# Three later norms of the residual: squares summed beside the residual's updates, root and inverse on [token, tile], reordering inside the dense stage

## The reference

```python
def _rmsnorm(x, g):
    x32 = x.astype(F32)
    y = x32 * lax.rsqrt(jnp.mean(x32 * x32, axis=-1, keepdims=True) + RMS_EPS)
    return y.astype(x.dtype) * g
def _modulate(h, shift, scale):
    return h * (1.0 + scale) + shift
...
    xl = xl + ml[2] * yl                                   # after the mixer
    hl = _modulate(_rmsnorm(xl, norm_g[i, 1]), ml[3], ml[4])
    xl = xl + ml[5] * ffn(hl)                              # after the feed-forward part
```

## Time and profile before

| | us |
|---|---|
| median of three runs | 2930.53 (2927.93 to 2930.65) |
| the profiled execution, its own time | 2932.93 |
| its span in the trace | 2930.9 |
| PE busy in the span | 2728.1 (93%) |
| DVE, ACT, POOL busy | 1048.0, 644.9, 520.1 |
| granted PE clock, mean | 0.958 |

### The profile page before, as it was taken

The page is one execution under the profiler, slowest core; times in us unless marked ns, Lnnn a source line. Parts: engine busy times, 40 slices in busy tenths (PEclk is TensorE's granted clock), DMA queues, the critical chain, the costliest instruction groups (busy, mean ns, idle before and its releaser), DMA issues. The chain is left out here.

```text
span 2930.9 us, 46270 instructions
## 1 busy us (share of the span) xinstructions
PE 2728.1 (93%) x18862; PEld 1829.9 (62%) x18863; DVE 1048.0 (36%) x2314; ACT 644.9 (22%) x1362; POOL 520.1 (18%) x466
## 2 busy tenths in 40 slices
PE   6699999796999999987999999999886999999997
PEld 6355555453555555554776677766635887688774
DVE  5244544416776664012444344443402110010100
ACT  0344544302222220004223232232102111010000
POOL 0111111003332224211333122331100010000000
PEclk6899999898999999998999999999887999999999
DMA  6142241202333333100111101110018997495731
GB/s 222 45 121 63 63 126 42 89 1 86 102 113 114 114 117 82 49 11 22 31 31 31 30 2 31 31 30 9 7 52 301 348 321 221 159 296 163 251 108 29
DMA packets 309234, 297.73 MB, mean 102 GB/s; under 512 B 5712, under 2 KB 268880, under 8 KB 308944
## 3 DMA queue, kind: packets, MB, share of 16 engines
q1 hardware_dynamic: 303024, 273.30, 30.4%
q0 software_dynamic: 4896, 17.83, 2.3%
q10 hardware_dynamic: 1152, 4.19, 0.4%
HBM read 281.14 MB, written 12.58 MB: 100 GB/s over the span
## 5 line engine op out<-in xcount | busy, mean ns | idle before, releaser
L1601 PE MATMUL bank<-work,weight_ring 128*128 128x128 f32 (+1 forms) x2048 | 315.4, 317 | 6.1 <-ACT work L1651 6.1
L2014 PE MATMUL bank<-hidden,weight_ring 128*128 128x512 f32 (+1 forms) x768 | 310.2, 538 | 1.8 <-ACT work L2336 1.8
L1601 PEld LDWEIGHTS bank<-work,weight_ring 128*128 128x128 f32 x2048 | 291.8, 193 | 27.7 <-issue 8.1
L601 PE MATMUL bank<-weight_ring,hidden 128*128 128x384 f32 x760 | 266.5, 495 | 4.9 <-ACT work L730 4.6
L1147 PE MATMUL bank<-hidden,weight_ring 128*128 128x384 f32 x704 | 238.2, 492 | 18.4 <-issue 18.4
L1268 DVE SCALAR_TENSOR_TENSOR weight_ring<-weight_ring,silu_c 128x256 f32<-128x256 f32 x308 | 217.8, 748 | 5.5
L601 PEld LDWEIGHTS bank<-weight_ring,hidden 128*128 128x128 f32 x760 | 137.9, 191 | 109.0 <-ACT work L730 16.6
L1147 PEld LDWEIGHTS bank<-hidden,weight_ring 128*128 128x128 f32 x704 | 133.1, 192 | 107.2 <-issue 20.6
L2014 PEld LDWEIGHTS bank<-hidden,weight_ring 128*128 128x128 f32 x768 | 135.5, 190 | 82.8 <-issue 68.7
L1147 PE MATMUL bank<-weight_ring 128*128 128x384 f32 x528 | 182.4, 496 | 0.3 <-DVE work L1276 0.3
L1756 DVE TENSOR_TENSOR work<-work,bank 128x128 f32<-128x128 f32 (+1 forms) x88 | 29.7, 337 | 426.0 <-ACT work L1656 426.0
(11 more groups left out here) (330 smaller groups left out, 3775.5 us busy)
## 6 DMA issues: line engine op xcount, KB each, us to landing
weight_ring<-in_moe_w_in SPq DMA_DIRECT2D x64, 1024.0 KB, 10.4
weight_ring<-in_ada_w SPq DMA_DIRECT2D x38, 1024.0 KB, 5.2
weight_ring<-in_ffn_w_in SPq DMA_DIRECT2D x44, 512.0 KB, 4.9
hidden<-in_moe_w_out SPq DMA_DIRECT2D x8, 2816.0 KB, 10.5
residual<-in_moe_w_out SPq DMA_DIRECT2D x8, 2816.0 KB, 16.1
work<-in_moe_w_in SPq DMA_DIRECT2D x16, 1024.0 KB, 8.8
weight_ring<-in_na_w_qkv SPq DMA_DIRECT2D x24, 512.0 KB, 7.7
weight_ring<-in_gdn_w_qkv SPq DMA_DIRECT2D x24, 512.0 KB, 5.4
```

The costliest lines, as they stand in the source:

```text
L601: mm = nc.tensor.matmul(m.psum[6][:, 0:3 * P], m.H[:, k, t * P:(t + 1) * P], weights(u)[:, k, :], start=(k == 0), stop=(k == KD - 1))
L1601: mm = nc.tensor.matmul(B[c % 4][:, ab * HALF:ab * HALF + N], w[:, ab, k, (c % 2) * P:(c % 2 + 1) * P], XG[:, k, 0:N], start=(k == 0), sto ...
L2014: mm = nc.tensor.matmul(B[b][:, c0:c0 + t1 - t0], W[:, s, k, :], m.H[:, k, t0:t1], start=(k == 0), stop=(k == KD - 1))
```

## The change

Norm n0 stays as it is. For n1, n2 and n3:

- ScalarE squares each group of the residual as soon as VectorE's additions to it are done, inside the projection's block or inside the dense stage. GpSimd adds the squares of groups 1 to 6 (in order of completion) to those of the first in `m.sq_sum`; the last group's squares stay in `m.sq`. Both are [128, 768]. They take the place of a buffer `silu_c_wide`, which now is a part of the same memory.
- `norm_apply` takes the place of `norm_modulate`. For each tile of 128 tokens TensorE makes two matmuls with the squares as the stationary operand and one column of 1/1024 as the moving one, so that the mean square of a token stands on its partition: [128, 6] for 768 tokens. ScalarE takes the root (after a one-element root at the start of the block), VectorE the inverse, both on [128, 6] ([128, 4] in n3). TensorE spreads each column over all partitions: stationary operand is the column, broadcast, and the moving one the identity. VectorE multiplies the residual by it, straight from PSUM and into `m.H`, and ScalarE scales and shifts `m.H` in place.
- `reorder` is gone. In the dense stage ScalarE copies each completed group's latents in the new order into `m.sq`, copies them back into the residual, and squares them from `m.sq`.

```diff
@@ -171,6 +171,8 @@
     m = Core()
...
     m.norm_sems = None
+    m.sq_sems = None
+    m.spread_sem, m.spread_base = None, 0
...
     m.sc = sb("silu_c", 2 * KD)[:, :]
-    m.sc32 = sb("silu_c_wide", 32 * KD)[:, :].rearrange("p (k v) -> p k v", k=KD)
+    stat = sb("square_sums", 2 * TOK)
+    m.sq_sum, m.sq = stat[:, 0:TOK], stat[:, TOK:2 * TOK]
+
+    m.sc32 = stat[:, 0:32 * KD].rearrange("p (k v) -> p k v", k=KD)
...
+def square_sums(m):
+    if m.sq_sems is None:
+        m.sq_sems = semaphores(m, "norm", "squared collected")
+        m.sq_base = [0, 0]
+    sems = m.sq_sems + m.sq_base
+    m.sq_base = [m.sq_base[0] + KD, m.sq_base[1] + KD - 2]
+    return sems
+def collect_squares(m, pool, sems, e, first=0):
+    squared, collected, squared_0, collected_0 = sems
+    pool.wait_ge(squared, squared_0 + e + 1)
+    if e > 1:
+        pool.wait_ge(collected, collected_0 + e - 1)
+    m.nc.gpsimd.tensor_tensor(m.sq_sum[:, first:TOK], m.sq_sum[:, first:TOK], m.sq[:, first:TOK], ALU.add).then_inc(collected, 1)
+def norm_apply(m, layer, norm, first=0, ahead=None):
+    nc = m.nc
+    if m.spread_sem is None:
+        m.spread_sem, = semaphores(m, "norm", "spread")
+    _, _, summed, root, inverted, scaled, hidden = m.norm_sems
+    _, _, summed_0, root_0, inverted_0, scaled_0, hidden_0 = m.norm_base
+    spread, spread_0 = m.spread_sem, m.spread_base
+    tiles = range(first // P, TOK // P)
+    rs = cut(m, 0, TOK // P)
+    warm = cut(m, TOK // P, 1)
+    parts = [(CTX, TOK, 0)] + ([(0, CTX, 1)] if first == 0 else [])
+    n = len(parts)
+    used = (0, 0, 1, 2, 1, KD * n, KD * n)
+    m.norm_base = [b + u for b, u in zip(m.norm_base, used)]
+    m.spread_base += n
+    with nc.Block() as block:
+        if ahead:
+            @block.sync
+            def _(sp):
+                ahead(sp)
+        @block.tensor
+        def _(pe):
+            for t in tiles:
+                for src in (m.sq_sum, m.sq):
+                    mm = nc.tensor.matmul(m.psum[0][:, t:t + 1], src[:, t * P:(t + 1) * P], const(m, C_MEAN, 1), start=(src is m.sq_sum),
+                                          stop=(src is m.sq))
+            mm.then_inc(summed, 1)
+            pe.wait_ge(inverted, inverted_0 + 1)
+            for b, (t0, t1, _) in enumerate(parts):
+                for t in range(t0 // P, t1 // P):
+                    mm = nc.tensor.matmul(m.psum[1 + b][:, t * P - t0:(t + 1) * P - t0], rs[:, t:t + 1].to_broadcast([P, P]), const(m, C_IDENT),
+                                          start=True, stop=True)
+                mm.then_inc(spread, 1)
+        @block.scalar
+        def _(act):
+            nc.scalar.activation(warm, const(m, C_EPS, 1), ACT.Sqrt).then_inc(root, 1)
+            act.wait_ge(summed, summed_0 + 1)
+            nc.scalar.activation(rs[:, first // P:], m.psum[0][:, first // P:TOK // P], ACT.Sqrt, bias=const(m, C_EPS, 1)).then_inc(root, 1)
+            for k in range(KD):
+                for b, (t0, t1, v) in enumerate(parts):
+                    act.wait_ge(scaled, scaled_0 + k * n + b + 1)
+                    nc.scalar.activation(m.H[:, k, t0:t1], m.H[:, k, t0:t1], ACT.Identity, bias=m.MOD[:, layer, 3 * norm, k, v:v + 1],
+                                         scale=m.MODA[:, layer, norm, k, v:v + 1]).then_inc(hidden, 1)
+        @block.vector
+        def _(dve):
+            dve.wait_ge(root, root_0 + 2)
+            nc.vector.reciprocal(rs[:, first // P:], rs[:, first // P:]).then_inc(inverted, 1)
+            for k in range(KD):
+                for b, (t0, t1, _) in enumerate(parts):
+                    dve.wait_ge(spread, spread_0 + b + 1)
+                    nc.vector.tensor_tensor(m.H[:, k, t0:t1], m.X[:, k, t0:t1], m.psum[1 + b][:, 0:t1 - t0], ALU.mult).then_inc(scaled, 1)
...
+    sums = square_sums(m)
+    squared, collected, _, collected_0 = sums
     with nc.Block() as block:
+
+        @block.scalar
+        def _(act):
+            for g in range(KD):
+                act.wait_ge(added, (g + 1) * len(parts))
+                if g > 1:
+                    act.wait_ge(collected, collected_0 + g - 1)
+                nc.scalar.activation((m.sq if g else m.sq_sum)[:, first:TOK], m.X[:, g, first:TOK], ACT.Square).then_inc(squared, 1)
+
+        @block.gpsimd
+        def _(pool):
+            for g in range(1, KD - 1):
+                collect_squares(m, pool, sums, g, first)
...
                 pool.wait_ge(*loaded(r, 1))
                 pool.wait_ge(product, out_done(r, "P2"))
                 nc.gpsimd.tensor_tensor(b, b, a, ALU.subtract).then_inc(weights_ok, 1)
+                for e in range(max(1, 2 * r - 2), 2 * r):
+                    collect_squares(m, pool, sums, e)
+            collect_squares(m, pool, sums, KD - 2)
...
                     nc.scalar.activation(sa[:, 1], sa[:, 1], ACT.Silu).then_inc(silu_ok, 1)
+
+
+            order = m.sq[:, CTX:TOK]
+            for e in range(KD):
+                r, row = divmod(e, 2)
+                g = r + PAIRS * row
+                act.wait_ge(added, len(OUT) * r + OUT.index(("P3", "P4")[row]) + 1)
+                if e > 1:
+                    act.wait_ge(collected, collected_0 + e - 1)
+                if e == 1:
+                    act.wait_ge(squared, sums[2] + 1)
+                at = 4 * FK + 4 + 2 * e
+                nc.scalar.copy(order.rearrange("p (r c) -> p r c", c=GRID_C), m.X[:, g, CTX:TOK].rearrange("p (c r) -> p r c", r=GRID_R))\
+                    .then_inc(copied, 1)
+                act.wait_ge(copied, at + 1)
+                nc.scalar.copy(m.X[:, g, CTX:TOK], order).then_inc(copied, 1)
+                act.wait_ge(copied, at + 2)
+                to = m.sq if e else m.sq_sum
+                nc.scalar.activation(to[:, CTX:TOK], order, ACT.Square)
+                nc.scalar.activation(to[:, 0:CTX], m.X[:, g, 0:CTX], ACT.Square).then_inc(squared, 1)
...
-def reorder(m):
-
-    nc = m.nc
-    copied, = semaphores(m, "reorder", "copied")
-    back, = semaphores(m, "reorder", "back")
-    tmp = cut(m, 0, KD * LAT).rearrange("p (k t) -> p k t", k=KD)
-    with nc.Block() as block:
-
-        @block.vector
-        def _(dve):
-            for k in range(KD):
-                nc.vector.tensor_copy(tmp[:, k, :].rearrange("p (r c) -> p r c", c=GRID_C),
-                                      m.X[:, k, CTX:TOK].rearrange("p (c r) -> p r c", r=GRID_R)).then_inc(copied, 1)
-
-        @block.scalar
-        def _(act):
-            for k in range(KD):
-                act.wait_ge(copied, k + 1)
-                nc.scalar.copy(m.X[:, k, CTX:TOK], tmp[:, k, :]).then_inc(back, 1)
...
         norm_modulate(m, "n0", 0, 0, ahead=attention_ahead(m))
         neighbourhood_attention(m, ahead=projection_ahead(m, "no", dram["na_w_o"]))
         project_to_residual(m, "no", 0, 0)
-        norm_modulate(m, "n1", 0, 1, ahead=swiglu_ahead(m))
+        norm_apply(m, 0, 1, ahead=swiglu_ahead(m))
         swiglu(m)
-        reorder(m)
-        norm_modulate(m, "n2", 1, 0, ahead=delta_net_ahead(m))
+        norm_apply(m, 1, 0, ahead=delta_net_ahead(m))
         delta_net(m)
         project_to_residual(m, "go", 1, CTX, load=projection_ahead(m, "go", dram["gdn_w_o"]))
-        norm_modulate(m, "n3", 1, 1, first=CTX)
+        norm_apply(m, 1, 1, first=CTX)
         experts(m)
```

More of the change, by code:

```diff
@@ L1036, in swiglu @@
     UP_DONE = CREDIT + FK * len(UP)
-    loads = {}
+    sums = square_sums(m)
+    squared, collected, _, collected_0 = sums
     def out_done(r, name):
```

## The result

The changed kernel takes 2891.78 us (median of 4 runs, 2889.23 to 2895.84), the kernel before, in the same series, 2930.59: a ratio of 0.9863, interval [0.9837, 0.9889], 39 us less. The forecast was 2897.1, so 5.3 us too high, and 2891.78 lies within its range of 2886 to 2907. The profiled execution took 2893.03, its span is 2891.1.

A forecast was written before the change was run, and what follows sets the result against it. TensorE, busy for 93% of the span, was taken as the bound, with 90 us of norm gaps on the path. Gains of 10.6, 15.9 and 6.9, together 33.4 us, took the median from 2930.53 to 2897.1; range 2886 to 2907.

The forecast's parts named there:

- Squares and copies: Last group's squares after the last addition, in n2 behind two copies: 0.88, 2.44, 0.67 us in n1, n2, n3.
- Edge to the sums: From the last instruction of a block to TensorE's first matmul of the sums: 0.61 us in each norm.
- Sums: Short matmuls over channels, 24 instructions (n3: 16) at 0.11 or 0.21 us: 3.9, 5.0, 3.4, plus 0.19 latency and hop.
- Root and inverse: In each norm, root 0.30 and inverse 0.18 on [128, 6], with hops 0.56 us.
- Spreading: TensorE spreading the latents in each norm, eight instructions of 128 columns: 2.0 us at 1.2 GHz, with hop 2.05.
- First product: VectorE's first product from PSUM in each norm: 0.68 us for 512, with hop 0.73.
- Scaling: ScalarE sets the pace as before: 9.68 us in n1 and n2, 5.75 in n3.
- tails: From scaling's end to the next stage's first matmul: 1.58 us before the dense stage, 0.61 before delta net and experts.
- Cover in the dense stage: GpSimd idles 22.67 us between rounds; the added work takes 5.8, so some 17 us are left.
- the fast clock: In all three norms the clock stays up through sums and spreading: 41.7 us gained, 2888.8; chance 0.1.
- Longer short steps: Each norm's eleven hand-overs cost 0.2 us, not 0.04; with other slow cases gain 24.8, time 2905.7; chance 0.1.
- A clock that stays down: Next stages begin with longer stretches at 1.2 GHz; 30 us in each would give 2942 us; chance 0.03.

The follow-up runs named there:

- the second profile: The unchanged changed kernel, run again and profiled on the chip of later runs: median 2891.74 us, ratio 0.9868 to the kernel before.
- the narrow form: Kernel before, with sums, root and inverse on [token, tile] in n1, n2, n3, squares still taken inside the norm: 2942.35 us, ratio 1.0041.
- the first narrow run: Kernel before, with sums, root and inverse on [token, tile], squares inside the norm, `start` set for each tile of group 0, output wrong: ratio 1.003.

## Why the prediction was right

Its mechanism held step by step: the chain is the one that it listed, and the dense stage hides the reordering. The forecast was 3.3 us too small in the gaps (33.4 against 36.7), and 5.3 too small by the second profile (38.7). By its own terms, in n1, n2, n3 of the first:

- *Squares and copies* (0.88, 2.44, 0.67): 0.88, 2.76, 0.66. The strided copy takes 1.12, not 0.63. Here the row of before, VectorE's copy, misled: one engine's copy was no price for another's. The rule of 16-byte lines that the prediction weighed (the Trainium skill, "SBUF — State Buffer", section "Door 1: The DMA port swizzle") pointed the right way for ScalarE, and of the 0.6 that the prediction put on it 0.5 came. VectorE's copy with the same step took 0.62 and shows no such cost, so the rule doesn't tell which engine pays.
- *Edge to the sums* (0.61 each): 0.31, 0.30, 0.31. It was taken from the delta net's and the experts' first matmul, which start 0.6 behind the scaling here too; what takes the other 0.3 there isn't shown. 0.9 of the error.
- *Sums* (with latency and hop 4.09, 5.19, 3.59): 2.85, 4.06, 3.18. The clock was up for all of n1's, for 1.4 us of n2's and 0.4 of n3's, longer than forecast. 2.8 of the error. The 25 ns that the prediction cites (the Trainium skill, "TensorE: Matmul & The Clock Gate", section "Back-to-back issue gap") don't hold for this run of matmuls: 2.81 / 24 = 0.117 at full clock. The same section gives its table for the isolated gap and says that it counts too little where each matmul has its weight load, as each has here.
- *Root and inverse* (0.56): 0.54 in n1. *Spreading* (2.05): 2.12; its own 0.21 each would give 8 x 0.21 + 0.17 + 0.05 = 1.90, so the 2.0 in the sum was a slip to the good side. *First product* (0.73): 0.72. *Scaling* (9.68, 9.68, 5.75) and *tails* (1.58, 0.61, 0.61): 9.68, 9.68, 5.75 and 1.55, 0.61, 0.60.
- *Cover in the dense stage*: 17 forecast, 16.6 measured; TensorE without a gap.

Of the rivals, the fast clock (41.7 gained) is half true: in the first profile n1's sums were fast and the spreading slow, in the second n3's sums and spreading were fast as well, and its 38.7 lies nearer to that rival than to the forecast, as the time of 2891.78 lies nearer to the rival's 2888.8 than to 2897.1. A chance of 0.1 was too little for it. That the forecast lay as near as it did is in part luck: which of the sums and spreadings the fall of the clock meets changes from execution to execution, and the prediction had one fixed point for each. Longer short steps: no, hops stay at 0.03 to 0.05. A clock that stays down: it is 0.50 for some 4 to 6 us at each start, as before. What the prediction did not price is the parts by themselves, and they are not additive: the narrow form loses 9 us without the early squares, where the expectation of the first narrow run had it gain 20. The time's 39 us hold 36.7 to 38.7 from the gaps. The rest can't be attributed: in the 14 profiles of all kernels the projection before n1 begins its additions anywhere from 574.9 to 583.0 us, behind stages that none of them changed, and takes 76.17 us for them in each.

## What to carry to other kernels

Between blocks with barriers, count the chain behind the last producer, not the engines' work: moving squares to idle engines as their inputs complete brought two thirds of the gain in the gaps here. A reduction that makes a statistic narrow spares the wide root and inverse, but 96 short matmuls cost more than 32 wide ones, and 24 cost little; shorten their list first. When TensorE idles and then does short work, price it at both levels of the clock, since the fall meets another instruction in each execution. Filling the idle time brought 1.2 us in the delta net, and nothing in the dense stage, where TensorE then waits for GpSimd.

## What the runs showed of the hardware

- After the same 2.34 us of idling in n1, and with TensorE busy without a pause, the clock stayed at 1.00 through 32 wide matmuls of the kernel before (660 to 670 us) and fell 2.5 us into the 96 short ones of the narrow form, which ran at 0.53 on average. A short matmul with its weight load takes 0.117 us per instruction at full clock and 0.21 at half.
- With `start` on each column of a PSUM bank while groups take turns over the columns, the output was off by 0.07 (relative); with `start` on the first column alone it was not. That `start` makes the next accumulating matmul overwrite the bank's other columns fits this, and was not read out.
- ScalarE's float32 copy of 512 takes 1.12 us with a step of 8 elements in the read and 1.08 with a step of 64 in the write, against 0.62. VectorE's with the step of 8 takes 0.62.
- The end of the unchanged stages before n1's projection varies by 8 us from profile to profile, more than most of the steps studied here; gaps in the timeline resolve steps of 1 us, which the medians of these runs can't, but for the fall of the clock, which moved n3's gap by 2.1 us between two profiles of the changed kernel.
